# Gated attention outputs turned by VectorE and DMA instead of TensorE, for six of eight heads of the last layer

## Chip, cores and metric

One Trainium2 chip, one of its cores. The metric is the device time of one execution of the whole program in microseconds; lower is better. The median of 3 runs before the change is 2311.38 us (2311.08 to 2311.39).

## What is computed

Two blocks on 256 tokens of 2048 channels. The first is a mixer, a cross attention and a gated feed-forward layer. The second is a convolution layer and then a differential-attention layer, which is the one that matters here:

```python
def _diff_layer(x, k, v, norm_g, w_in, q_norm_g, lam_p, subln_g, w_out, layer_idx):
    ...
    q = _rms_norm(q, q_norm_g) * (DIFF_HEAD_DIM ** -0.5)
    ...
    o = _diff_attention(q, k, v, lam)          # 8 heads, each 2 maps of 128 and 256 values wide
    o = _rms_norm(o, subln_g) * (1.0 - lam_init)
    o = o.reshape(bsz, s, DIFF_V) * jax.nn.silu(z)
    return x + o @ w_out
```

Everything is fp32. The last product, `o @ w_out`, needs the gated output with its 2048 channels along the partitions, while the attention leaves it with the tokens along them, so it has to be turned.

## The kernel before

**Halves and slots.** All large products are walked as one line of 704 "halves" of weights, two blocks of 128 rows by 512 columns each (one product of 32 columns apart). For each half ScalarE rounds the fp32 weights in RAW to fp32r (WHI), VectorE takes the remainder (WLO; GpSimd does so for a part of the convolution layer), and TensorE multiplies: high by high, high by low and low by high, for two halves of the tokens and two blocks, 12 matmuls of 128x512. There are four buffers of WHI and WLO, so ScalarE may round half h+3 when TensorE is through with half h-1 (`ahead`, line 493). SyncE loads the weights, four pieces of two halves ahead.

**Steps behind halves.** Everything else is written out by hand as steps that each engine carries out, in its own program order, behind a given half: `put` for the whole kernel, and for the last layer `diff_put(s, ...)`, which counts slots from the first half of "dq" (line 643 on). Slots 0 to 31 are the query product, 32 to 63 the product for the gate z, and 64 to 71 the first column block of the output product "do". At a slot an engine first prepares weights (rounding or remainder of half s+3) and then does its steps; TensorE multiplies half s and then does its steps. Behind slots 39, 47, 55 and 63 ScalarE also evicts a block of z with Silu into DZ, after its steps.

**Attention.** There are 16 units n (head n//2, token half n%2). The steps of unit n lie at slots from 12+3n on: `ds` the scores on TensorE; one slot later `dexp`, a maximum on VectorE and two exponentials on ScalarE; at +2 `dp`, three VectorE instructions that mix the two maps; at +3 `dt`, TensorE turns the result; +4 `dcopy` on ScalarE; +5 `do`, the product with the values; +6 `dsquare`, the squares on ScalarE and then a scale and a power on GpSimd; +7 `dscale`, VectorE writes the scaled output to XD. Scores read queries and keys from DQT and DKT.

**The turn around the change.** Head h is multiplied by its gate on VectorE (`gated`, slot 43 to 67) and one slot later turned (`oT`, slots 44, 47, 50, 53, 59, 62, 66, 68). `oT` is four 128x128 transposes on TensorE (line 100) into a PSUM bank, two ScalarE instructions that scale and round to Ohi, and two VectorE instructions for the remainder Olo. Ohi shares its place with the keys (DKT) and Olo with the queries (DQT). "do" needs chunks 2p and 2p+1 of Ohi and Olo at its part p, that is at slot 64+p.

**The other way of turning.** For several earlier stages the kernel already turns without TensorE: `swap` (VectorE, line 1528) turns a block of 128x512 in 32x32 squares, two instructions of line 117, into a buffer of 4 KB per partition; `move` (line 665) then lets SyncE and GpSimd issue eight DMAs each, within SBUF, that carry the squares to their places (line 138); `moved_hi` and `moved_lo` read them from there. All swaps stand in the list SWAPS, and one waits until the move of the one before has landed. The last swap before the change is that of the first query block.

Of the kernel before, what the change touches and what calls it, by code (L numbers as in the profile page):

```python
# [164 lines left out]
def flat(ap):  # L165
    return ap.rearrange("p a c -> p (a c)")
# [6 lines left out]
def build_program(nc, I, C, out):  # L173
# [4 lines left out]
    def at(name, kb, shape, dt=F32):  # L178
# [4 lines left out]
    X = at("X", 0, [2, D])  # L183
# [8 lines left out]
    AR = 122  # L192
# [80 lines left out]
             "x3": (at("T3", AR + 64, [1024]), at("B3", AR + 68, [1024])),  # L273
             "x4": (at("T4", AR + 80, [1024]), at("B4", AR + 48, [1024])),
             "x5": (at("T5", AR + 80, [1024]), at("B5", AR + 54, [1024])),
             "ff": (at("TF", AR + 80, [1024]), flat(AC))}
    SWAPS = [("x2", 0), ("x2", 1), ("xk", 0), ("x2", 2), ("xk", 1), ("x2", 3), ("xk", 2), ("xk", 3)]
    SWAPS += [("xq", i) for i in range(3)] + [("x3", i) for i in range(4)] + [("ff", i) for i in range(11)] + [("x4", i) for i in range(4)] + [("x5", i) for i in range(4)]
    SWAPS += [("dk", i) for i in range(4)] + [("dq", 0)]

    X5_HOMES = (SWAP["x5"][1], at("B5b", AR + 58, [1024]))

# [3 lines left out]
    def blocks_home(stage, i):  # L286
        if stage == "xk":
            return flat(XK[:, 4 * i:4 * i + 4, :])
        if stage == "x5":
            return X5_HOMES[i % 2][:, :]  # L290
        return SWAP[stage][1][:, :]

    def landing(stage, i):
# [364 lines left out]
    for h in range(8):  # L658
        s = (44, 47, 50, 53, 59, 62, 66, 68)[h]
        diff_put(s - 1, ("gated", h))  # L660
        diff_put(s, ("oT", h))
    for i in range(1, 4):
        put(("dq", i + 1) if i < 3 else ("dz", 0), 0, ("head", "dq", i))

# [466 lines left out]
    def act_program(engine):  # L1131
# [160 lines left out]
        def step(what, *a):  # L1292
# [118 lines left out]
            elif what == "yT":  # L1411
                e.wait_ge(*full(("down", 6, 3)))
                for q in (4 * k, 4 * k + 2):
                    e.wait_ge(*of("pa", ("yT", q)))
                    e.activation(YT[:, q:q + 2, PAD:PAD + T], kc(pa.ap(("yT", q))[:, :])).then_inc(*done("yT", q))
            elif what == "zT":
                for q in (4 * k, 4 * k + 2):
                    e.wait_ge(*of("pa", ("zT", q)))
                    e.activation(ZT[:, q:q + 2, 0:T], kc(pa.ap(("zT", q))[:, :])).then_inc(*done("zT", q))
            elif what == "tap0":  # L1420
                tap0(k)
            elif what == "copy":
                e.wait_ge(*of("tap", 2 * k + 1, CW - 1))
                e.activation(CV[:, 2 * k:2 * k + 2, :], kc(pb.ap(("taps", k))[:, :])).then_inc(*done("copied", k))
            elif what == "provisional":
                e.wait_ge(*of("pa", ("provisional",)))
                e.activation(MU[:, :], pa.ap(("provisional",))[:, 0:T], scale=1.0 / (4 * P)).then_inc(*done("provisional", 0))
            elif what == "square":
                e.wait_ge(*(of("centred_pool", k) if k < 2 else of("centred", k)))
                if k > 2:  # L1430
                    e.wait_ge(*of("added", k - 2))
                o = SQ[:, 2 * (k % 2):2 * (k % 2) + 2, :] if k else SSQ
                e.activation(o, CV[:, 2 * k:2 * k + 2, :], AF.Square).then_inc(*done("squared", k))
            elif what == "stats":
                dm = cols("dm", 2)
                e.wait_ge(*of("variance", 0))
                e.activation(DIAG[:, 0, :], IDN[:, :], scale=dm[:, 0:1])
                e.activation(DIAG[:, 1, :], IDN[:, :], scale=dm[:, 1:2]).then_inc(*done("diag_mean", 0))
            elif what == "spread_rstd":
                rs = cols("rs", 2)  # L1440
                e.wait_ge(*of("rstd", "y"))
                e.activation(DIAG[:, 2, :], IDN[:, :], scale=rs[:, 0:1])
                e.activation(DIAG[:, 3, :], IDN[:, :], scale=rs[:, 1:2]).then_inc(*done("diag_rstd", 0))
            elif what == "silu_y":
                silu_y(k)
            elif what == "y_hi":
                y_hi(k)
            elif what == "x5T":
                e.wait_ge(*full(("cz", 3)))
                moved_hi("x5", k)  # L1450
            elif what == "x5bT":
                moved_hi("x5b", k)
            elif what == "mask":
                e.wait_ge(*of("d_mrow", 0))
                e.activation(MASK, MROW).then_inc(*done("mask", 0))
            elif what == "dexp":
                nk = P * (k % 2 + 1)
                v, o = pa.ap(("ds", k))[:, 0:2 * nk].rearrange("p (m c) -> p m c", m=2), diff_exps(k)
                mx, sm = cols(("dmax", k % 4), 2), cols(("dsum", k % 4), 2)
                if k > 1:  # L1460
                    e.wait_ge(*of("pa", ("dt", k - 2)))
                e.wait_ge(*of("diff_max", k))
                for mp in range(2):
                    i = e.activation(o[:, mp, 0:nk], v[:, mp, :], AF.Exp, bias=mx[:, mp:mp + 1], accum_out=sm[:, mp:mp + 1])
                i.then_inc(*done("diff_exp", k))
            elif what == "dcopy":
                nk = P * (k % 2 + 1)
                if k > 1:
                    e.wait_ge(*of("pb", ("do", k - 2)))
                e.wait_ge(*of("pa", ("dt", k)))  # L1470
                e.activation(diff_turned(k)[:, 0:nk], pa.ap(("dt", k))[:, 0:nk]).then_inc(*done("diff_T", k))
            elif what == "dsquare":
                h, t = k // 2, k % 2
                e.wait_ge(*of("pb", ("do", k)))
                e.activation(XD[:, t, h * T:(h + 1) * T], pb.ap(("do", k))[:, 0:T], AF.Square,
                             accum_out=cols(("dss", k % 4), 1)[:, 0:1]).then_inc(*done("diff_sq", k))
            elif what == "oT":
                e.wait_ge(*of("sg", 0))
                t_hi("o", 2 * k, pa, "pa", ("o", 2 * k))

        e.wait_ge(*of("half", 0))
        e.activation(cols("begin", 1), HALF[:, 0:1]).then_inc(*done("act_begun", 0))
# [18 lines left out]
    def dve_program(engine):  # L1501
# [26 lines left out]
        def swap(stage, i):  # L1528
            n = SWAPS.index((stage, i))
            if n:  # L1530
                for landed_blocks in landing(*SWAPS[n - 1]):
                    e.wait_ge(*landed_blocks)
            home_free = {("xq", 0): full(("xkv", 7)), ("dk", 0): full(("co", 3)), ("dq", 0): full(("dv", 3)),
                         ("x2", 0): of("mem_sq", 1), ("x3", 0): of("pa", ("att", 3)), ("x5", 0): of("pa", ("zT", 14)), ("ff", 0): of("pa", ("qxT", 14))}
            if i == 0 and (stage, i) in home_free:
                e.wait_ge(*home_free[stage, i])
            made = {"ff": "up", "xk": "xkv", "xq": "xq", "dk": "dk", "dq": "dq"}
            e.wait_ge(*(evicted((made[stage], i)) if stage in made else of("x_add", stage, i, 1)))
            for t in range(2):
                a = {"ff": AC, "xk": NT, "xq": NT, "dk": ND, "dq": ND}[stage][:, t, :] if stage in made else X[:, t, i * 512:(i + 1) * 512]  # L1540
                m = e.turn_blocks(turned_blocks(stage, t), a.rearrange("p (k q c) -> p q k c", k=4, q=4))
            m.then_inc(*done("swapped", stage, i))

# [337 lines left out]
        def step(what, *a):  # L1881
# [163 lines left out]
            elif what == "dexp":  # L2045
                nk = P * (k % 2 + 1)
                e.wait_ge(*of("pa", ("ds", k)))
                e.reduce(cols(("dmax", k % 4), 2), pa.ap(("ds", k))[:, 0:2 * nk].rearrange("p (m c) -> p m c", m=2), AL.max, negate=True) \
                    .then_inc(*done("diff_max", k))
            elif what == "dp":  # L2050
                diff_weights(k)
            elif what == "dscale":
                h, t = k // 2, k % 2
                e.wait_ge(*of("rstd", ("diff", k)))
                e.tensor_scalar(XD[:, t, h * T:(h + 1) * T], pb.ap(("do", k))[:, 0:T], cols(("r", ("diff", k % 4)), 1)[:, 0:1], AL.mult) \
                    .then_inc(*done("diff_o", k))
            elif what == "gated":
                s = slice(k * T, (k + 1) * T)
                e.wait_ge(*of("diff_o", 2 * k + 1))
                e.wait_ge(*evicted(("dz", k // 2)))  # L2060
                e.tensor_tensor(XD[:, 0, s], XD[:, 0, s], DZ[:, 0, s], AL.mult)
                e.tensor_tensor(XD[:, 1, s], XD[:, 1, s], DZ[:, 1, s], AL.mult).then_inc(*done("gated", k))
            elif what == "oT":
                e.wait_ge(*of("sg", 0))
                t_lo("o", 2 * k, pa, ("o", 2 * k))

        begun = 0
        for h, (name, part, last) in enumerate(line):
# [338 lines left out]
```

## Time and profile before

| | us |
|---|---|
| median of 3 runs | 2311.38 |
| lowest, highest | 2311.08, 2311.39 |
| the profiled execution: its time | 2312.47 |
| the profiled execution: its span | 2310.6 |

The profile is of one execution. Its span reaches from the first to the last instruction; the 1.87 us between span and time lie around it. The page lists busy time per engine, the span in 40 slices, the DMA queues, the chain of work that ended last, and groups of instructions. Times in the rows further down are microseconds from the start of the span. In this trace slot 44 ends at about 2155, slot 64 begins at about 2219, and the last matmul ends at about 2307.5.

### The profile page before, as it was taken

How to read it: one execution, taken by the hardware profiler on the slowest of the kernel's cores; microseconds unless marked ns; L12 is line 12 of the kernel's file. 1: busy time of each engine (PE TensorE's matmuls, PEld its weight loads, DVE VectorE, ACT ScalarE, POOL GpSimd, SP SyncE). 2: the span in 40 equal slices, each digit the busy share in tenths (PEclk: the TensorE clock that was granted, in tenths of full speed). 3: DMA queues.
4: the chain of work that ended last, by engine and by line, in shares of the span. 5: the costliest groups of instructions: out<-in, count | busy, mean ns of one | idle time of the engine just before them, and what ended most of it. 6: DMA issues, size and time to landing. Idle time of an engine off the chain costs nothing.

```text
span 2310.6 us, 26507 instructions
## 1 busy us (share of the span) xinstructions
PE 2303.0 (100%) x10418; PEld 1898.8 (82%) x10418; DVE 1422.9 (62%) x1939; ACT 1118.1 (48%) x1452; POOL 494.0 (21%) x567
## 2 busy tenths in 40 slices
PE   9999999999999999999999999999999999999999
PEld 7778888888888888888888888888888888888887
DVE  6687756644556555554455555679994765466564
ACT  6444555544335444443344444544556554444653
POOL 1001011300102100100000101159987322022100
PEclk9999999999999999999999999999999999999999
DMA  9566466765546666565566566655655676554454
GB/s 335 191 195 201 149 225 208 235 222 184 171 147 222 206 228 199 192 227 186 197 201 201 196 219 212 201 197 168 200 182 182 199 241 218 187 187 152 158 172 138
DMA packets 252380, 458.17 MB, mean 198 GB/s; under 512 B 19658, under 2 KB 39813, under 8 KB 251552
## 3 DMA queue, kind: packets, MB, share of 16 engines
q1 hardware_dynamic: 238608, 432.13, 56.2%
q0 software_dynamic: 13648, 24.35, 3.8%
q8 instruction: 82, 1.34, 0.2%
q14 instruction: 42, 0.34, 0.0%
HBM read 431.79 MB, written 2.10 MB: 188 GB/s over the span
## 4 chain that ended last, share of the span: by engine, by line
PE 95%; DVE 2%; ACT 1%; DMA 1%; issue 1%; SPq 0%; POOL 0%; DVEq 0%; ACTq 0%
PE ps L97 94%; PE ps L100 1%; DVE WLO L109 1%; ACT WHI L103 0%; DMA RAW<-in_w_in 0%; SPq L138 0%; DMA B<-T 0%; POOL B L138 0%; DVE MIX L109 0%; DMA B5b<-T 0%; ACT ps L103 0%; DVE T L117 0%; ACT L103 0%; DVE UU L109 0%; DVE HS L109 0%
## 5 line engine op out<-in xcount | busy, mean ns | idle before, releaser
L109 DVE TENSOR_TENSOR WLO<-RAW,WHI 128x1024 fp32r<-128x1024 f32 x701 | 851.5, 1221 | 700.6 <-ACT WHI L103 697.3
L103 ACT ACTIVATE WHI<-RAW 128x1024 fp32r<-128x1024 f32 x793 | 836.2, 1059 | 867.7 <-PE ps L97 861.8
L97 PE MATMUL ps<-WHI,Ahi 128*128 128x512 f32 x1904 | 750.8, 395 | 0.3 <-DVE WLO L109 0.3
L97 PE MATMUL ps<-WHI,Alo 128*128 128x512 f32 x1904 | 741.7, 390 | 0.0
L97 PE MATMUL ps<-WLO,Ahi 128*128 128x512 f32 x1904 | 741.4, 390 | 0.0
L97 PEld LDWEIGHTS ps<-WHI,Ahi 128*128 128x128 f32 x1904 | 358.6, 188 | 76.5 <-issue 2.3
L97 PEld LDWEIGHTS ps<-WLO,Ahi 128*128 128x128 f32 x1904 | 358.7, 188 | 75.4 <-issue 2.3
L97 PEld LDWEIGHTS ps<-WHI,Alo 128*128 128x128 f32 x1904 | 358.5, 188 | 75.0
L109 POOL TENSOR_TENSOR WLO<-RAW,WHI 128x1024 fp32r<-128x1024 f32 x92 | 219.0, 2417 | 53.0 <-ACT WHI L103 52.6
L120 DVE SCALAR_TENSOR_TENSOR ps<-YT,GC,ps 128x256 f32<-128x256 f32 x480 | 188.8, 482 | 8.0 <-ACT ps L103 8.0
L138 POOL DMA_DIRECT2D AC<-TF x88 | 46.4, 535 | 562.0 <-DVE TF L117 559.1
L97 PE MATMUL ps<-WHI,Bhi 128*128 128x512 f32 x384 | 150.3, 391 | 0.0
L97 PE MATMUL ps<-WHI,Blo 128*128 128x512 f32 x384 | 149.4, 389 | 0.0
L97 PE MATMUL ps<-WLO,Bhi 128*128 128x512 f32 x384 | 149.4, 389 | 0.0
L114 POOL TENSOR_SCALAR ST<-ST 128x1 f32<-128x1 f32 (+3 forms) x53 | 21.8, 412 | 549.4 <-DVE ST L123 258.6
L97 PE MATMUL ps<-WHI,Fhi 128*128 128x512 f32 x352 | 136.9, 389 | 0.0
L97 PE MATMUL ps<-WLO,Fhi 128*128 128x512 f32 x352 | 136.9, 389 | 0.0
L97 PE MATMUL ps<-WHI,Flo 128*128 128x512 f32 x352 | 136.9, 389 | 0.0
L138 POOL DMA_DIRECT2D B<-T x112 | 59.4, 538 | 218.5 <-DVE T L117 206.7
L97 PE MATMUL ps<-WHI,Dhi 128*128 128x512 f32 x256 | 102.6, 401 | 0.0
L97 PE MATMUL ps<-WHI,Dlo 128*128 128x512 f32 x256 | 100.1, 391 | 0.0
L97 PE MATMUL ps<-WLO,Dhi 128*128 128x512 f32 x256 | 99.9, 390 | 0.0
(328 smaller groups left out, 2216.3 us busy)
## 6 DMA issues: line engine op xcount, KB each, us to landing
RAW<-in_w_gate_up SPq DMA_DIRECT2D x88, 1024.0 KB, 5.1
RAW<-in_a_w_in SPq DMA_DIRECT2D x48, 1024.0 KB, 5.1
RAW<-in_w_down SPq DMA_DIRECT2D x44, 1024.0 KB, 5.0
RAW<-in_w_in SPq DMA_DIRECT2D x39, 1024.0 KB, 5.2
RAW<-in_w_xkv SPq DMA_DIRECT2D x32, 1024.0 KB, 5.6
RAW<-in_w_kv SPq DMA_DIRECT2D x32, 1024.0 KB, 5.7
RAW<-in_b_w_in SPq DMA_DIRECT2D x32, 1024.0 KB, 5.4
RAW<-in_w_out SPq DMA_DIRECT2D x16, 1024.0 KB, 5.0
```

Source lines behind the costliest of these rows:

```text
L97: return self.e.matmul(o, l, r, start=start, stop=stop, skip_group_check=True)
L100: return self.e.transpose(o, i, ident)
L103: return self.e.activation(o, i, func, scale=scale, **kw)
L109: return self.e.tensor_tensor(o, a, b, op)
L114: return self.e.tensor_scalar(o, a, s1, s2, op0, op1)
L120: return self.e.scalar_tensor_tensor(out=o, in0=a, scalar=s, in1=b, op0=op0, op1=op1)
L138: return self.e.dma_start(o, i)
```

## The change

Heads 0 to 5 are no longer turned on TensorE. At slots 47, 53 and 62 a swap "o" 0, 1 and 2 takes two gated heads (512 columns of XD) each, as soon as the second of them is gated. The squares lie in a buffer TO (where ND was) and are moved to places that queries and keys no longer in use have left: DQT 8 to 11, DKT 8 to 11 and DQT 12 to 15. Two and three slots later `moved_hi` and `moved_lo` read four chunks in two steps. SyncE and GpSimd issue the moves at the slot of the swap, because their programs carry out every "swap" step. Heads 6 and 7 stay on TensorE.

```diff
-             "ff": (at("TF", AR + 80, [1024]), flat(AC))}
+             "ff": (at("TF", AR + 80, [1024]), flat(AC)), "o": (at("TO", AR + 80, [1024]), None)}
...
-    SWAPS += [("dk", i) for i in range(4)] + [("dq", 0)]
+    SWAPS += [("dk", i) for i in range(4)] + [("dq", 0)] + [("o", i) for i in range(3)]
...
+        if stage == "o":
+            return flat((DQT[:, 8:12, :], DKT[:, 8:12, :], DQT[:, 12:16, :])[i])
...
     for h in range(8):
         s = (44, 47, 50, 53, 59, 62, 66, 68)[h]
         diff_put(s - 1, ("gated", h))
-        diff_put(s, ("oT", h))
+        if h >= 6:
+            diff_put(s, ("oT", h))
+        elif h % 2:
+            diff_put(s, ("swap", "o", h // 2))
+            diff_put(s + 2, ("oM", 2 * h - 2))
+            diff_put(s + 3, ("oM", 2 * h))
...
+            elif what == "oM":
+                e.wait_ge(*of("sg", 0))
+                moved_hi("o", k)
...
-                         ("x2", 0): of("mem_sq", 1), ...}
+                         ("x2", 0): of("mem_sq", 1), ...,
+                         ("o", 0): of("pa", ("dqT", 14))}
...
-            e.wait_ge(*(evicted((made[stage], i)) if stage in made else of("x_add", stage, i, 1)))
+            if stage == "o":
+                e.wait_ge(*of("gated", 2 * i + 1))
+                e.wait_ge(*of("pa", ("ds", (11, 11, 15)[i])))
+            else:
+                e.wait_ge(*(evicted((made[stage], i)) if stage in made else of("x_add", stage, i, 1)))
...
-                a = {...}[stage][:, t, :] if stage in made else X[:, t, i * 512:(i + 1) * 512]
+                a = {...}[stage][:, t, :] if stage in made \
+                    else (XD if stage == "o" else X)[:, t, i * 512:(i + 1) * 512]
...
+            elif what == "oM":
+                e.wait_ge(*of("sg", 0))
+                moved_lo("o", k)
```

## Rows read from the trace of the kernel before

**Rows 1.** The page: busy us by engine, and TensorE's granted clock by slice.

```profile
PE 2303.0 (100%) x10418; PEld 1898.8 (82%) x10418; DVE 1422.9 (62%) x1939; ACT 1118.1 (48%) x1452; POOL 494.0 (21%) x567
...
PEclk9999999999999999999999999999999999999999
```

**Rows 2.** Whom TensorE waited for, whole span: us in total, times, longest.

```profile
PE ps L97 <- DVE WLO L109: 1.6, 2, 1.3
PE ps L97 <- issue: 1.1, 1, 1.1
```

**Rows 3.** Chain that ended last, from 1980 us: start, us, what (L100 transposes).

```profile
2155.67 0.44 PE ps L100 x4
...
2233.96 73.51 PE ps L97 x324
```

**Rows 4.** Instructions on XD: TensorE transposes, duration ns min/median/max.

```profile
L100 PE MATMUL ps<-IDN,XD x32: 270/272/275, 2155.5 to 2233.7; 128*128 128x128 f32 x32
```

**Rows 5.** Timeline of DVE, POOL and SP at the last swap: start, us, engine.

```profile
2038.75 1.30 DVE L117 STREAM_TRANSPOSE TDQ<-ND 128x512 f32<-128x512 f32 x2
...
2040.35 4.30 POOL L138 DMA_DIRECT2D BDQ<-TDQ  x8 [3.15 <-DVE TDQ L117]
...
2040.08 5.95 SPq L138 DMA_DIRECT2D BDQ<-TDQ  x8
...
2047.37 1.14 DVE L114 TENSOR_SCALAR DQT<-BDQ,GC 128x256 f32<-128x256 f32 x4 [2.80 <-DMA BDQ<-TDQ]
```

**Rows 6.** Timeline of VectorE, slots 47 to 50.

```profile
2165.86 0.48 DVE L120 SCALAR_TENSOR_TENSOR TMP<-TMP,ST 128x256 f32<-128x256 f32 x1
2167.21 0.88 DVE L120 SCALAR_TENSOR_TENSOR Olo<-ps,ST,Ohi 128x256 fp32r<-128x256 f32 x2 [0.87 <-ACT Ohi L103]
...
2173.72 0.48 DVE L113 TENSOR_SCALAR XD<-ps,ST 128x256 f32<-128x256 f32 x1 [0.44 <-POOL ST L109]
2174.12 0.41 DVE L123 TENSOR_REDUCE ST<-ps 128x2 f32<-128x256 f32 x1
...
2177.50 0.15 DVE L132 RECIPROCAL ST<-ST 128x1 f32<-128x1 f32 x1
```

**Rows 7.** GpSimd: a scale and a power; all powers from 2140 to 2240 (ns min/median/max).

```profile
2158.45 0.93 POOL L114 TENSOR_SCALAR ST<-ST 128x1 f32<-128x1 f32 x1 [5.97 <-ACT XD L103]
2159.47 0.55 POOL L109 TENSOR_TENSOR ST<-ST 128x1 f32<-128x1 f32 x1
...
L109 POOL TENSOR_TENSOR ST<-ST x8: 548/550/1507, 2147.9 to 2220.0; 128x1 f32<-128x1 f32 x8
```

**Rows 8.** Timeline of ScalarE: moved chunks of an earlier stage, then slots 49 to 56.

```profile
1851.12 0.91 ACT L103 ACTIVATE Ahi<-B5b,GC 128x256 fp32r<-128x256 f32 x2 [1.92 <-DMA B5b<-T]
...
2174.57 0.37 ACT L103 ACTIVATE GC<-ps,ST 128x128 f32<-128x128 f32 x1 [0.98 <-DVE ST L123]
...
2175.27 1.05 ACT L103 ACTIVATE WHI<-RAW 128x1024 fp32r<-128x1024 f32 x1
...
2193.58 1.28 ACT L103 ACT_TABLE_LOAD   x1
...
2196.03 2.00 ACT L103 ACTIVATE WHI<-RAW 128x1024 fp32r<-128x1024 f32 x2
```

**Rows 9.** Timeline of TensorE: `dt` of units 12 and 14, `oT` of head 6.

```profile
2179.23 0.28 PE L100 MATMUL ps<-IDN,GC 128*128 128x128 f32 x1
...
2199.30 0.27 PE L100 MATMUL ps<-IDN,GC 128*128 128x128 f32 x1
...
2227.43 0.60 PE L100 MATMUL ps<-IDN,XD 128*128 128x128 f32 x4
```

**Rows 10.** Timeline of VectorE: end of slot 56 (`dp` of unit 14), slots 62 and 65.

```profile
2198.72 0.35 DVE L120 SCALAR_TENSOR_TENSOR GC<-GC,ST 128x128 f32<-128x128 f32 x1
...
2213.78 1.23 DVE L109 TENSOR_TENSOR WLO<-RAW,WHI 128x1024 fp32r<-128x1024 f32 x1 [0.62 <-ACT WHI L103]
...
2225.08 0.75 DVE L109 TENSOR_TENSOR XD<-XD,DZ 128x256 f32<-128x256 f32 x2
```

More of the change, by code:

```diff
@@ L1533, in swap @@
             home_free = {("xq", 0): full(("xkv", 7)), ("dk", 0): full(("co", 3)), ("dq", 0): full(("dv", 3)),
-                         ("x2", 0): of("mem_sq", 1), ("x3", 0): of("pa", ("att", 3)), ("x5", 0): of("pa", ("zT", 14)), ("ff", 0): of("pa", ("qxT", 14))}
+                         ("x2", 0): of("mem_sq", 1), ("x3", 0): of("pa", ("att", 3)), ("x5", 0): of("pa", ("zT", 14)), ("ff", 0): of("pa", ("qxT", 14)),
+                         ("o", 0): of("pa", ("dqT", 14))}
             if i == 0 and (stage, i) in home_free:
@@ L1537, in swap @@
             made = {"ff": "up", "xk": "xkv", "xq": "xq", "dk": "dk", "dq": "dq"}
-            e.wait_ge(*(evicted((made[stage], i)) if stage in made else of("x_add", stage, i, 1)))
+            if stage == "o":
[3 more added lines that the diff above has]
+                e.wait_ge(*(evicted((made[stage], i)) if stage in made else of("x_add", stage, i, 1)))
             for t in range(2):
-                a = {"ff": AC, "xk": NT, "xq": NT, "dk": ND, "dq": ND}[stage][:, t, :] if stage in made else X[:, t, i * 512:(i + 1) * 512]
+                a = {"ff": AC, "xk": NT, "xq": NT, "dk": ND, "dq": ND}[stage][:, t, :] if stage in made \
+                    else (XD if stage == "o" else X)[:, t, i * 512:(i + 1) * 512]
                 m = e.turn_blocks(turned_blocks(stage, t), a.rearrange("p (k q c) -> p q k c", k=4, q=4))
```

## Prediction, made before the changed kernel was run

> **What bounds the kernel.** I read the page first. TensorE is busy over the whole span, VectorE 62%, ScalarE 48%, and the granted clock is full in every slice, its 2.4 GHz level [rows 1]. The list of waits then shows that TensorE hardly waits for anyone: 1.6 us for VectorE and 1.1 us for "issue" in 2310.6 us [rows 2]. So every instruction taken off TensorE comes off the end, and every new wait of TensorE is added to it. The chain of waits gives the price of the transposes in question: the four of a head hold TensorE for 0.44 us between weight matmuls [rows 3]. The timelines around the last existing swap [rows 5] and around slots 47 to 66 [rows 6 to 10] show what the other engines will be asked to do instead, and how early they are today.
>
> **Removed from TensorE.** Six heads at four transposes at 0.11 us: 6 x 0.44 = 2.64 us [rows 3]. The same transposes have a duration of 272 ns each [rows 4], but they overlap one another and the matmuls around them. The chain counts what they delay, and I take it.
>
> The Trainium skill (TensorE: Matmul & The Clock Gate, Part 4: PE-mode transpose) puts a 128x128 transpose at about 275 ns in one kernel, which is the row's duration. By that figure the gain would be 6.6 us instead of 2.64.
>
> **Removed from ScalarE and VectorE, and put back.** Two roundings and two remainders per head stay as they are, only their source moves from PSUM to SBUF: 0.91 us for two roundings of moved chunks [rows 8], 0.88 us for two remainders [rows 6]. New are two VectorE turns per swap, 1.30 us [rows 5], three times. VectorE has the time on average; the question is what stands behind them.
>
> **Added on the queues.** Per swap GpSimd issues eight DMAs, 4.30 us, beginning 0.3 us after the turn; SyncE issues eight too, 5.95 us, and the data is in place 7.3 us after the turn ended (2040.05 to 2047.37) [rows 5]. On SyncE only weight loads are queued behind them, four pieces or eight halves of 12 matmuls ahead, 8 x 12 x 73.51/324 = 21.8 us [rows 3]; 5.95 us of lateness fits into that, so I cost it at nothing. On GpSimd the scale and power of `dsquare` stand behind them. These take 1.57 us with their gap (2158.45 to 2160.02) [rows 7]. So GpSimd delivers at +4.6 +1.6 = 6.2 us after the turn at the earliest, and VectorE's `dscale`, one slot after `dsquare`, waits for it. That `dscale` stands ahead of the maximum of a later unit.
>
> The last existing swap cost TensorE the 1.1 us of "issue" in [rows 2], at the time when VectorE waited for the moved queries of [rows 5], on which the first scores depend. A swap can stall TensorE.
>
> **Swap 0 (slot 47).** TensorE runs 0.44 us earlier here, after one `oT` less, so `dp` of unit 11 ends at 2165.85 (was 2165.86 + 0.45 [rows 6]), and the turn ends at 2167.15 = A. Then: dscale at A+6.2; maximum 0.40 later; exponentials 0.45 after that, A+7.05; they take 0.70 (2174.57 to 2175.27 [rows 8]), A+7.75. Now the new rounding (landed since A+7.3) 0.87, A+8.6. VectorE, in order, holds at the remainder of the moved chunks for it: 0.88, A+9.5. Then `gated` 0.7, the weights' remainder 1.15 [rows 10] (both a little under the row, since the next instruction starts before the end of the last), three instructions of `dp` 0.8 [rows 6, 10]: A+12.1 = 2179.25. TensorE's `dt` of unit 12 was at 2179.23 [rows 9]; three `oT` less it would be there at 2177.9. **Stall 1.3 us.**
>
> **Swap 1 (slot 53).** VectorE now works without a gap from 2179.2: remainder 0.88, two weights' remainders 2.3, dscale 0.4, maximum 0.7; exponentials 0.9, rounding 1.1, remainder 1.15, `dp` of unit 13 0.9, turn 1.3: B = 2188.8. Up to the moved rounding all is as above, B+8.6. But this is slot 55, where ScalarE must still load a table and evict z, together 2.45 (2193.58 to 2196.03), before it rounds the weights, 0.96 [rows 8], and VectorE takes its remainder, 1.15, and `dp` of unit 14, 0.8: B+14.1 = 2202.9. `dt` of unit 14 was at 2199.30 [rows 9], without further stall now 2198.9. **Stall 4.0 us.** Before, this chain ended at 2199.07 [rows 10], 0.2 us before TensorE came to it.
>
> **Swap 2 (slot 62).** All is 3.6 us later, less 0.44 for head 4: remainder at 2213.78 + 3.15 [rows 10] = 2216.9, turn ends at 2219.4, landed at 2226.7. ScalarE rounds the moved chunks to 2227.5, the weights to 2228.5; VectorE then the weights' remainder 2229.6, the second moved one 2230.5, `gated` of head 6 2231.3. TensorE's `oT` of head 6 was at 2227.43 [rows 9], now ready at 2230.1. **Stall 1.2 us.** From there on only full halves follow, with three buffers of lead, and the 324 matmuls of the tail [rows 3] keep their pace.
>
> **Sum.** -2.64 + 1.3 + 4.0 + 1.2 = +3.9 us. For the profiled execution 2312.47 + 3.9 = 2316.4 us; the median of the runs is 1.09 lower than that execution, so 2311.38 + 3.9 = **2315.3 us**. A measurement of this kernel tells 0.2% from nothing, 4.6 us: the bounds are 2306.8 and 2316.0, and the forecast is within them, near the upper.
>
> Two prices are not shown in this place. A burst of eight issues on GpSimd while VectorE works: between the 4.30 us of GpSimd and the 5.95 us of SyncE [rows 5]; I take GpSimd's own. GpSimd's scale and power right behind a burst: between 1.57 and 0.93 + 0.09 + 1.51 = 2.5 us [rows 7]; I take the first, as the median power took 0.55 us.
>
> **Rivals.**
> *The stalls are covered* (chance 0.20). If VectorE's lead absorbs the waits, as around the 39 earlier swaps, where TensorE's waits are 2.7 us in all [rows 2], only the gain remains, with at most half the stalls: 2308.7 to 2311.9 us. For it speaks that every step has a slot of slack by design; against it, that `dt` of unit 14 has next to none and that GpSimd was idle beside the earlier swaps [rows 5], with no `dscale` behind them.
> *GpSimd behind its DMAs is slow* (chance 0.22, slower). If the power takes 1.51 instead of 0.55 us [rows 7] after a burst of issues, swaps 0 and 1 both pay 0.9 us more: 2315.3 + 1.8 = 2317.1 us. It decides from 0.7 us of extra stall in the sum on. Against it: of the eight powers of these slots the median took 0.55 [rows 7].
> *The clock falls* (chance 0.03, slower). TensorE would idle 4.0 us in one go, three times more than anywhere before. If it goes on at 1.2 GHz for one half, whose 12 matmuls take 12 x 73.51/324 = 2.7 us [rows 3] at full clock, that adds 2.7 us: 2318.0. No stretch of this trace shows the lower level, so only a stall as long as that can tell.
> The Trainium skill (TensorE: Matmul & The Clock Gate, Why this matters for your kernels) asks to keep gaps between bursts of matmuls short, or the clock goes back to half; the trace before has no gap that would test it.
> *A transpose costs its full duration* (chance 0.03, faster). 24 x 0.272 = 6.5 us [rows 4] with the stalls covered gives 2304.9 us. Against it: the chain's 0.44 for four [rows 3].
> *The change does nothing* (0.02): if heads were still turned on TensorE, 2311.4. The diff leaves no room for it.
>
> **How the numbers follow.** The forecast case holds 0.50: +1.8 to +5.5 us, 2313.2 to 2316.9, of which a tenth of all chance lies above 2316.0. Slower: 0.22 + 0.03 + 0.10 = 0.35. Faster by over 0.2%: 0.03. Within: 0.62. The range runs from 2309.5, into the covered case, to 2318.2, past the slow GpSimd.
>
> **What would show it.** In the profile after: TensorE's transposes on XD fall from 32 to 8. TensorE waits for VectorE's TMP/GC (the mixed maps) at slots 51 and 57 with gaps of about 1.3 and 4 us, and for XD before head 6 with about 1.2. GpSimd has three bursts of eight DMAs of 4.3 us each in front of a late scale and power; VectorE's XD from `dscale` waits for GpSimd some 2 to 4 us. The step is wrong if GpSimd's burst ends well before `dscale` is due, if the moved chunks land much later than 7.3 us (then the landing, not GpSimd, sets it), or if the gaps sum to less than 2.6 us, which makes the kernel faster. If TensorE waits for WLO instead, the lead of three halves was used up, and the sum is wrong upwards.

## The result, and the profile after

The changed kernel takes 2316.15 us (median of 13 runs, 2313.84 to 2317.92) against 2311.39 us (13 runs, 2310.72 to 2312.92): +4.76 us, a ratio of 1.0021 with a 95% interval of 1.0014 to 1.0028. The forecast was 2315.3 us, in a range of 2309.5 to 2318.2. The measured median lies 0.15 us above 2316.0, the upper bound of what the prediction counted as no change; it had given 0.35 to the side above it. The runs of the changed kernel lie over 4.1 us, those before over 2.2 us; a part of that spread has a cause of its own, below.

The page after, busy us by engine, beside [rows 1]:

```profile
PE 2301.9 (100%) x10394; PEld 1895.7 (82%) x10394; DVE 1425.8 (62%) x1945; ACT 1117.9 (48%) x1452; POOL 504.3 (22%) x591
```

TensorE has 24 instructions less, VectorE 6 more, GpSimd 24 more, its half of the moves. Busy time barely moves. The instructions on XD after, beside [rows 4]:

```profile
L100 PE MATMUL ps<-IDN,XD x8: 270/273/328, 2230.1 to 2236.4; 128*128 128x128 f32 x8
```

Of 32 transposes 8 are left, so the change does what it says. Whom TensorE waits for from 2140 us on, after (us in total, times, longest); before there was the last of the three lines alone:

```profile
PE ps L100 <- DVE GC L120: 3.7, 2, 3.1
PE ps L100 <- DVE XD L109: 1.2, 1, 1.2
PE ps L100 <- DVE TMP L120: 0.2, 1, 0.2
```

Three new waits (two of the first line, one of the second), at the three places of the forecast. The profiled execution of this kernel took 2315.23 us with a span of 2313.3. Its start is not comparable to the microsecond: at unit 9, ahead of all changed slots, it is already 1.64 us ahead of the one before (2146.70 against 2148.34 us), which is chance of a single execution: the one profiled before lies 1.09 us above the median of its kernel, this one 0.92 below. So I count from that transpose to the final addition (chain of waits, after, then the same before):

```profile
2146.70 0.44 PE ps L100 x2
...
2310.20 0.69 DVE X L109
```

```profile
2148.34 0.44 PE ps L100 x2
...
2307.49 0.69 DVE X L109
```

That is 2310.20 - 2146.70 = 163.50 us. Before it was 2307.49 - 2148.34 = 159.15 us: +4.35 us within the changed stretch.

TensorE's timeline after, the units 12 and 14 and head 6, beside [rows 9]:

```profile
2177.07 0.33 PE L100 MATMUL ps<-IDN,GC 128*128 128x128 f32 x1 [0.60 <-DVE GC L120]
2177.23 1.03 PE L97 MATMUL ps<-DKT,DQT 128*128 128x256 f32 x4
...
2199.97 0.47 PE L100 MATMUL ps<-IDN,GC 128*128 128x128 f32 x1 [3.05 <-DVE GC L120]
2200.24 1.91 PE L97 MATMUL ps<-DKT,DQT 128*128 128x256 f32 x4
2201.59 0.78 PE L97 MATMUL ps<-MASK 128*128 128x256 f32 x1
2202.17 0.63 PE L97 MATMUL ps<-WHI,Dhi 128*128 128x512 f32 x1
2202.59 0.53 PE L97 MATMUL ps<-WLO,Dhi 128*128 128x512 f32 x1
2202.96 0.40 PE L97 MATMUL ps<-WHI,Dlo 128*128 128x512 f32 x1
...
2230.09 0.66 PE L100 MATMUL ps<-IDN,XD 128*128 128x128 f32 x4 [1.23 <-DVE XD L109]
```

Taken against the places of [rows 9], 1.64 us earlier and 0.44 us less per head removed, and with what came before taken off, the three stalls are 0.8, 3.3 and 1.4 us. That is some 0.2 us more than the idle times of 0.60, 3.05 and 1.23: matmuls that otherwise start 0.23 us apart and take 0.39 do not overlap across a wait.

Behind the long one there is something more. The four score matmuls after unit 14 take 1.91 us where they took 1.03 us elsewhere (at 2177.23 us, behind unit 12). Windows of five microseconds, after (columns: busy us and count of PE, PEld, DVE, ACT, POOL, then granted clock, DMA share, GB/s):

```profile
2195.00:2200.00 5.00, 1.95 (x10) 1.26 (x9) 2.29 (x6) 4.99 (x10) 0.00 (x0) 0.95 0.25 96
2200.00:2205.00 5.00, 5.00 (x17) 4.16 (x18) 4.64 (x8) 3.43 (x8) 2.03 (x2) 0.71 0.77 230
2205.00:2210.00 5.00, 5.00 (x23) 4.12 (x23) 2.72 (x5) 2.51 (x5) 0.55 (x2) 1.00 0.50 193
```

The granted clock is 0.71 between 2200 and 2205 us: a part of it at 1.2 GHz, after 3 us in which TensorE did nothing, and back at 2.4 GHz by 2205. From unit 14 to the third weight matmul behind it pass 2202.96 - 2199.97 = 2.99 us. Before, it was 2200.86 - 2199.30 = 1.56:

```profile
2199.30 0.27 PE L100 MATMUL ps<-IDN,GC 128*128 128x128 f32 x1
...
2200.86 0.40 PE L97 MATMUL ps<-WHI,Dlo 128*128 128x512 f32 x1
```

**The fall of the clock costs 1.4 us.** The idling before it does not make the difference: in the profiled execution of experiment 5, below, TensorE idles 2.54 us in this place, the clock is 1.00 in the windows around it, and the same stretch takes 2200.20 - 2198.58 = 1.62 us. The page's line by slices shows nothing of it, as a slice is 58 us long. By the Trainium skill (TensorE: Matmul & The Clock Gate, Why this matters for your kernels) long gaps between bursts of matmuls put the clock back to half; this trace agrees, with 0.71 behind a gap of 3.05 us.

The sum within the trace: 24 transposes -2.6 (measured below), stalls +5.5, clock +1.4, together +4.3, against +4.35. The stalls are themselves differences of places, so up to head 6 the sum closes by its making. What the trace shows beside it is that the idle times fit the stalls, and that nothing is added behind head 6.

Now the chain behind the 3.3 us, on three engines (timelines after, slots 53 to 56):

```profile
2185.10 1.30 DVE L117 STREAM_TRANSPOSE TO<-XD 128x512 f32<-128x512 f32 x2
...
2191.97 0.48 DVE L113 TENSOR_SCALAR XD<-ps,ST 128x256 f32<-128x256 f32 x1 [2.52 <-POOL ST L109]
2192.37 0.41 DVE L123 TENSOR_REDUCE ST<-ps 128x2 f32<-128x256 f32 x1
2194.46 0.88 DVE L120 SCALAR_TENSOR_TENSOR Olo<-DKT,ST,Ohi 128x256 fp32r<-128x256 f32 x2 [1.67 <-ACT Ohi L103]
2197.98 1.22 DVE L109 TENSOR_TENSOR WLO<-RAW,WHI 128x1024 fp32r<-128x1024 f32 x1 [2.64 <-ACT WHI L103]
```

```profile
2186.69 4.30 POOL L138 DMA_DIRECT2D DKT<-TO  x8 [4.21 <-DVE TO L117]
2191.03 0.27 POOL L114 TENSOR_SCALAR ST<-ST 128x1 f32<-128x1 f32 x1
2191.38 0.56 POOL L109 TENSOR_TENSOR ST<-ST 128x1 f32<-128x1 f32 x1
```

```profile
2193.52 0.90 ACT L103 ACTIVATE Ohi<-DKT,ST 128x256 fp32r<-128x256 f32 x2
2194.44 1.28 ACT L103 ACT_TABLE_LOAD   x1
2195.74 1.27 ACT L103 ACTIVATE DZ<-ps,ST 128x512 f32<-128x512 f32 x2
2196.89 1.05 ACT L103 ACTIVATE WHI<-RAW 128x1024 fp32r<-128x1024 f32 x1
```

It reads from top to bottom. The turn ends at 2186.40. GpSimd issues eight DMAs and only then does its scale and power, so VectorE's scaled output waits 2.52 us for it and the maximum of unit 14 comes at 2192.37, 6.0 us after the turn. ScalarE's exponentials (2192.82 to 2193.52) are followed by the moved rounding, then the table and the eviction of z, then the weights of the next half; VectorE waits for each of the two and mixes unit 14 at last, 13.5 us after the turn. The landing is not what ends last here: the moved rounding starts at 2193.52, at once behind the exponentials.

### The profile page after: what moved, and what is told of

Read it like the earlier page. It is cut to its first block, busy times and chain, and to the rows that moved or that the text cites. A ratio compares the mean times of both kernels' runs of the same rounds, so it can differ in the third digit from the quotient of the medians.

```text
span 2313.3 us, 26521 instructions
## 1 busy us (share of the span) xinstructions
PE 2301.9 (100%) x10394; PEld 1895.7 (82%) x10394; DVE 1425.8 (62%) x1945; ACT 1117.9 (48%) x1452; POOL 504.3 (22%) x591
## 4 chain that ended last, share of the span: by engine, by line
PE 93%; DVE 3%; ACT 2%; DMA 1%; issue 1%; POOL 1%; SPq 0%; DVEq 0%; ACTq 0%
PE ps L97 92%; DVE WLO L109 1%; PE ps L100 1%; ACT WHI L103 1%; SPq L138 0%; DMA RAW<-in_w_in 0%; DMA B<-T 0%; ACT L103 0%; POOL DKT L138 0%; POOL DQT L138 0%; DVE TO L117 0%; POOL B L138 0%; DVE MIX L109 0%; DMA DQT<-TO 0%; ACT ps L103 0%
```

## The experiments

All times are medians of 11 runs, beside 21 or 33 runs of the kernel before on the same chip (2311.40, 2311.36 and 2311.21 us in the three groups). Where a kernel leaves work out, as in experiments 2 to 4, its output is not the right one; such kernels serve for the time alone.

**1. The work on the transposes alone.** Kernel before, with this in TensorE's step:

```diff
             elif what == "oT":
                 e.wait_ge(*of("gated", k))
+                if k < 6:
+                    bank, free = pa.banks[len(pa.held) % 2], pa.held[len(pa.held) - 2]
+                    e.wait_ge(*of(*free))
+                    for j in range(2):
+                        for t in range(2):
+                            c = 2 * k + j
+                            e.transpose(bank[:, j * T + t * P:j * T + (t + 1) * P], XD[:, t, c * P:(c + 1) * P], IDN[:, :])
                 turn_nat("o", 2 * k, XD)
```

> The kernel before the change, with the 24 transposes of heads 0 to 5 done twice (the first time into the same bank, overwritten by the second). It measures the price of the removed work by itself. By the chain of waits a head costs 0.44 us (0.42 in the traces of the first experiments): +2.5 to +2.6 us, 2313.9 to 2314.0 us. Rival, that a transpose costs its duration of 272 ns: +6.5 us, 2317.9 us.

Measured 2313.99 us (2313.48 to 2315.54), ratio 1.0012 (1.0003 to 1.002): +2.63 us for 24 transposes, 0.44 us per head. TensorE's timeline shows eight where there were four in 0.60 us:

```profile
2154.12 1.04 PE L100 MATMUL ps<-IDN,XD 128*128 128x128 f32 x8
```

The price is the chain's: four more transposes add 1.04 - 0.60 = 0.44 us. The 272 ns of [rows 4] is the duration of one, of which the next covers more than half. By the Trainium skill's 275 ns (TensorE: Matmul & The Clock Gate, Part 4: PE-mode transpose) it would have been 6.6 us; the number agrees with the row and not with the cost in this place.

**2. The change without its swaps.**

```diff
-            diff_put(s, ("swap", "o", h // 2))
...
-    SWAPS += [("dk", i) for i in range(4)] + [("dq", 0)] + [("o", i) for i in range(3)]
+    SWAPS += [("dk", i) for i in range(4)] + [("dq", 0)]
...
+            if stage == "o":
+                e.wait_ge(*of("gated", k // 4 * 2 + 1))
+                e.wait_ge(*of("pa", ("ds", (11, 11, 15)[k // 4])))
```

> The changed kernel without the three swaps: no VectorE turns, no DMAs; the rounding and remainder of heads 0 to 5 stand in their new slots and read what lies in the places of old keys and queries (so the gated outputs of six heads do not reach the output product). My theory: the gain of the removed transposes is real and shows in full once the waits behind the swaps are gone, 2311.4 - 2.6 = 2308.8 us, no TensorE stall over 0.5 us in slots 44 to 68, and no fall of the granted clock. Rival, that the new places of the roundings alone upset VectorE's order: the stalls of 0.8 and 3.3 us at units 12 and 14 stay in part, 2310 us or more.

Measured 2309.36 us (2308.82 to 2311.01), ratio 0.9991 (0.9982 to 1.0): -2.04 us, 0.6 less than the gain that I expected. TensorE's waits from 2140 us on are the 0.2 us at unit 9 and one new:

```profile
PE ps L100 <- DVE GC L120: 0.4, 1, 0.4
```

So the gain is there, less 0.6 us. The one new wait, 0.44 us of idling and 0.2 around it, accounts for that; as I read it, it is the price of the new place of the roundings at unit 14, in front of the eviction of z. The rest of the loss comes with the swaps.

**3. The turns without the DMAs.**

```diff
     def move(e, stage, i, blocks):
+        if stage == "o":
+            return
...
-            for landed_blocks in landing(home, k // 4):
+            for landed_blocks in (landing(home, k // 4) if stage != "o" else [of("swapped", "o", k // 4)]):
...
-                for landed_blocks in landing(*SWAPS[n - 1]):
+                for landed_blocks in (landing(*SWAPS[n - 1]) if stage != "o" or i == 0 else ()):
```

> The changed kernel with VectorE's turns but without any of the 48 DMAs; the moved roundings wait for the turn alone (six heads' outputs do not reach the product). Theory: the stalls come from GpSimd's burst and the landing, not from VectorE's 1.3 us per swap, so the time is that of the kernel without swaps (2309.4 us) or up to 0.5 us more: 2309.4 to 2309.9 us, clock 1.00. Rival, VectorE as the bound: 2311 us or more, TensorE waiting for VectorE at units 12 and 14 by over 1 us.

Measured 2309.32 us (2308.7 to 2309.93), ratio 0.9991 (0.9982 to 1.0), with the same single wait of 0.4 us. Against experiment 2 VectorE's six turns cost nothing that shows. The whole difference to the changed kernel, 2316.15 - 2309.32 = 6.8 us, is the 48 DMAs: their issue, their landing and what the stall does to the clock.

**4. Without GpSimd's half of the moves.**

```diff
-        return [of(f"d_move{b}", stage, i, 3) for b in range(4)]
+        return [of(f"d_move{b}", stage, i, 3) for b in range(2 if stage == "o" else 4)]
...
-            elif what == "swap":
+            elif what == "swap" and k != "o":
                 move(e, *a, blocks=(2, 3))
```

> The changed kernel without GpSimd's half of the moves: SyncE issues its eight DMAs per swap as before, GpSimd none, and nobody waits for the missing half (half of the squares of six heads are missing). Rival, that GpSimd's scale and power behind its DMAs set the stall: the stalls at units 12 and 14 shrink by about 2 us each and the kernel falls to 2311 to 2312 us. My reading of the trace after: dscale becomes early, but the landing of SyncE's half, 7.3 us after the turn, holds the moved rounding at the same moment as before, so the two waits hide each other and the time stays at 2315 to 2316.5 us with the same stalls of about 0.8, 3.3 and 1.4 us.

Measured 2313.96 us (2312.63 to 2314.46), ratio 1.001 (1.0002 to 1.0019): 2.2 us less than the changed kernel, so the time I named is missed by 1 us, and the rival's by 2. The timeline of VectorE and that of ScalarE in slots 55 and 56 show why it is between them (the turn ends at 2186.70 here):

```profile
2190.07 0.41 DVE L123 TENSOR_REDUCE ST<-ps 128x2 f32<-128x256 f32 x1
2194.09 0.88 DVE L120 SCALAR_TENSOR_TENSOR Olo<-DKT,ST,Ohi 128x256 fp32r<-128x256 f32 x2 [3.61 <-ACT Ohi L103]
```

```profile
2193.15 0.91 ACT L103 ACTIVATE Ohi<-DKT,ST 128x256 fp32r<-128x256 f32 x2 [1.83 <-DMA DKT<-TO]
```

As I read it, the maximum comes 2.6 us earlier after the turn (3.4 instead of 6.0 us) and it hardly helps, because the rounding now waits for the landing. But SyncE's half alone lands 6.45 us after the turn, not 7.3, and the idle times shrink to 0.35 and 2.4 us with none at head 6. In the change the exponentials end 7.1 us after the turn (2193.52), here the landing comes at 6.45. Two waits end within a microsecond of each other; taking one away yields only the difference, and the mix of unit 14 comes 12.9 instead of 13.5 us after the turn.

**5. The roundings one slot later.**

```diff
-            diff_put(s + 2, ("oM", 2 * h - 2))
-            diff_put(s + 3, ("oM", 2 * h))
+            if h < 5:
+                diff_put(s + 3, ("oM", 2 * h - 2))
+                diff_put(s + 4, ("oM", 2 * h))
...
+        if h == 6:
+            diff_put(65, ("oM", 8))
+            diff_put(66, ("oM", 10))
...
+                e.wait_ge(*of("T_lo", "o", 2 * k - 2))
```

> The changed kernel with its swaps where they are, but the moved roundings and remainders one slot later, behind the mixes of units 12 and 14 (slots 50 and 51, 56 and 57) and behind the gating of head 6 (65 and 66). It takes the landing out of the way and leaves GpSimd's burst in front of the scale. By the trace after: the maximum 6.0 us after the turn, exponentials to 7.1, table and eviction 2.45, rounding and remainder of weights 2.1, mix 0.8: unit 14 at 12.5 instead of 13.6 us after the turn, and unit 12 not late at all. Stall 1.9 us at unit 14, none at unit 12, at most 0.3 at head 6: 2311.4 - 2.5 + 1.9 = 2310.8 us (2310.2 to 2311.6). Rival, that the place of the roundings alone made the stalls: 2309.2 us. Rival, that GpSimd's burst alone made them: 2314 us or more.

Measured 2313.3 us (2311.03 to 2314.57), ratio 1.0007 (0.9999 to 1.0016): 2.5 us more than I expected, and outside the range. The waits from 2140 us on are where I said, with the one at unit 12 and the one at head 6 gone and this one left:

```profile
PE ps L100 <- DVE GC L120: 2.5, 1, 2.5
```

It is 2.5 us where I had 1.9, and I had left out the clock: in eight of the 11 runs the mean granted clock is 0.999. Those eight lie at 2312.83 to 2314.57, the other three at 2311.03 (the profiled one), 2311.65 and 2311.70, near the forecast. VectorE's timeline shows the part that is GpSimd's alone, in slot 55:

```profile
2191.37 0.48 DVE L113 TENSOR_SCALAR XD<-ps,ST 128x256 f32<-128x256 f32 x1 [2.81 <-POOL ST L109]
```

So at unit 14 TensorE idles 3.05 us in the change, 2.4 without GpSimd's burst (experiment 4), 2.5 with the roundings behind the mix (here), and 0.4 without any DMA (experiment 3). Neither cause alone accounts for the stall; each hides most of the other.

**6. Without swap 1, and with swap 1 alone.** The first leaves heads 2 and 3 on TensorE, the second all the others (the list SWAPS is shortened to match):

```diff
-        if h >= 6:
+        if h >= 6 or h in (2, 3):
             diff_put(s, ("oT", h))
```

```diff
-        if h >= 6:
+        if h not in (2, 3):
             diff_put(s, ("oT", h))
```

> Heads 2 and 3 are turned on TensorE again as before the change; swaps 0 and 2 stay. Theory: swap 1 carries the long stall (3.3 us) and, behind it, the fall of the clock (1.4 us in the profiled run). Without it -16 transposes 1.76, +0.8 (unit 12) +1.4 (head 6): 2311.8 us (2311 to 2312.5), granted clock 1.00 from slot 44 to the end, and the spread over the runs as small as before the change (2 us or less). Rival, that each swap costs about a third: 2314.5 us.

> Only heads 2 and 3 by swap (slot 53), the other six heads on TensorE. Theory: -0.84 for eight transposes, a stall of about 2.8 us at unit 14 and, in most runs, the fall of the clock behind it, 1.4 us: 2314.7 us (2313.5 to 2315.5), in two levels 1.4 us apart according to the mean granted clock of the run. Rival, each swap costs a third of the loss: 2313 us, and the clock stays.

Without swap 1: 2313.72 us (2313.06 to 2314.81), ratio 1.0011 (1.0002 to 1.002), 1.9 us more than expected and outside the range; the rival's 2314.5 is nearer. TensorE's waits from 2150 us on:

```profile
PE ps L100 <- DVE XD L109: 2.9, 2, 1.5
```

One of the two is the known one at head 6. The other, 1.51 us, is new and stands at slot 50: with head 2 back on TensorE, its transposes wait for its gating, which VectorE does behind the remainder of swap 0. I had carried over only the stall at unit 12; the same lateness meets whatever stands next. It costs 1.7 us in place of the 0.8 at unit 12, which is 0.9 of the 1.9 us; the stall at head 6 is 0.4 longer than I had it. The clock is 1.00 in all 11 runs, and the spread is 1.75 us, as expected.

Swap 1 alone: 2314.45 us (2313.28 to 2315.15), ratio 1.0013 (1.0004 to 1.0022), as expected and 1.5 us above the rival, so swap 1 carries more than a third. It waits 2.6 us at unit 14, and the window behind it shows the clock:

```profile
2200.00:2205.00 5.00, 4.77 (x16) 3.93 (x17) 4.90 (x9) 3.43 (x8) 2.03 (x2) 0.67 0.66 220
```

The four runs with a mean clock of 1.000 lie at 2313.28 to 2314.64 (median 2313.5), the seven with 0.999 at 2314.14 to 2315.15 (median 2314.7): 1.2 us apart. The two levels overlap, since runs of one level differ by as much. Above the transposes that are saved, swap 1 alone costs 3.24 + 0.88 = 4.1 us, swaps 0 and 2 cost 2.32 + 1.76 = 4.1, and all three together 4.76 + 2.64 = 7.4: the costs of the swaps are not independent of each other.

**7. Other slots for the same work.**

```diff
-        s = (44, 47, 50, 53, 59, 62, 66, 68)[h]
+        s = (44, 47, 50, 53, 59, 60, 66, 68)[h]
...
-            diff_put(s, ("swap", "o", h // 2))
-            diff_put(s + 2, ("oM", 2 * h - 2))
-            diff_put(s + 3, ("oM", 2 * h))
+            w, m0, m1 = {1: (48, 51, 53), 3: (54, 57, 59), 5: (60, 63, 64)}[h]
+            diff_put(w, ("swap", "o", h // 2))
+            diff_put(m0, ("oM", 2 * h - 2))
+            diff_put(m1, ("oM", 2 * h))
```

> The same work as in the change at other slots: each swap one slot later, right behind GpSimd's scale and power (48, 54, and 60 with head 5 gated at 59), the moved roundings where VectorE has neither a maximum nor a mix ahead of TensorE (51, 53; 57, 59; 63, 64). Theory: all three stalls go, the gain of 2.6 us is left: 2308.8 us (2308 to 2310), clock 1.00. Rival, that the transfers themselves or VectorE's six extra turns cost time wherever they stand: 2311 us or more.

Measured 2309.99 us (2309.52 to 2310.44), ratio 0.9994 (0.9985 to 1.0003). The same transposes, turns and 48 DMAs, and 6.2 us less than the change. Nothing is left but one wait of 0.6 us at head 6, where I had expected none. This is also what speaks against the transfers or the turns as such: they are all still there. The next kernel has (43, 46, 49, 52, 57, 57, 64, 67) as slots of `gated`, swap 2 at 58, its roundings at 61 and 62, and a wait for the remainder of the chunks before, since the places overlap in time:

> The slots of e4_shifted, and the third pair earlier: heads 4 and 5 gated at slot 57, swap 2 at 58, its roundings at 61 and 62, head 6 gated at 64, so that neither the landing nor the eviction of z behind slot 63 stands in front of head 6. Theory: the last 0.6 us stall goes too, 2310.0 - 0.8 = 2309.2 us or a little less (2308.8 to 2309.4), no stall over 0.3 us in slots 44 to 68 besides the 0.2 us at unit 9. Rival, that the landing at slot 61 or swap 2's burst in front of the scale of unit 14 makes a new wait: 2310 us or more.

Measured 2309.22 us (2308.5 to 2311.61), ratio 0.9991 (0.9982 to 1.0): TensorE waits for no one behind unit 9, and -2.14 us of the possible 2.5 to 2.6 are there. Then the last two heads, gated together at slot 64 and moved to the place of the used values:

```diff
+    DVH = at("DVH", AR + 48, [4, T])
...
+            w, m0, m1 = {1: (48, 51, 53), 3: (54, 57, 59), 5: (58, 61, 62), 7: (64, 67, 68)}[h]
...
+                e.wait_ge(*(of("pa", ("ds", (11, 11, 15)[i])) if i < 3 else of("pb", ("do", 15))))
```

> As e7_all_waits_gone, and heads 6 and 7 too by VectorE and DMA: both gated at slot 64, swap 3 there, moved to the place of the used values, rounded at slots 67 and 68. The output product needs chunks 12 at slot 70, 14 at 71. Theory: another 2 x 0.42 us less, 2308.3 us (2308 to 2308.8). Rival, that the landing, 7.4 us or 2.7 halves after the turn, comes too late for the rounding and remainder before slot 70: 2309.5 us or more, with TensorE waiting for Olo or for the weights' remainder.

Measured 2308.2 us (2307.52 to 2309.03), ratio 0.9986 (0.9977 to 0.9994): **3.2 us faster than the kernel before and 8 us faster than the change.** All its 11 runs lie below the lowest of the 33 beside them (2310.60). For the two kernels before it the intervals reach 1.0 or past it, so their gains rest on the traces as much as on the times. TensorE's waits over the whole span hold nothing behind unit 9, whose 0.2 us were there before:

```profile
PE ps L97 <- DVE WLO L109: 1.7, 2, 1.5
PE ps L97 <- POOL ONE L135: 1.0, 1, 1.0
PE ps L97 <- DVE KN L106: 0.3, 1, 0.3
PE ps L97 <- issue: 0.3, 1, 0.3
PE ps L100 <- DVE TMP L120: 0.2, 1, 0.2
```

ScalarE does wait there for the last landing, 4.42 us, with nothing of TensorE's behind it but halves whose weights are ready:

```profile
2229.78 0.91 ACT L103 ACTIVATE Ohi<-DVH,ST 128x256 fp32r<-128x256 f32 x2 [4.42 <-DMA DVH<-TO]
```

## Why the prediction was right, and where its sizes were off

The sign, the places and, roughly, the size hold. Point by point:

- **The removed work**, 2.64 us: 2.63 by doubling it (experiment 1), and 2.57 within the same stretch of the trace of the second kernel of experiment 7, which has no new wait (2303.20 - 2146.62 = 156.58 against 159.15 us). Right.
- **The turns on VectorE at nothing**: right, experiment 3.
- **SyncE's eight DMAs at nothing**: after the change TensorE waits for no WLO and ScalarE for no RAW in slots 44 to 71. Right.
- **Swap 0**: 1.3 us forecast, 0.8 in the trace. The term at fault is GpSimd's scale and power behind its burst, for which I took 1.57 us; from their start to VectorE's scaled output it is 0.94 (2191.03 to 2191.97 at swap 1, 2170.12 to 2171.06 at swap 0). The rival that made them slow was the wrong way round.
- **Swap 1**: 4.0 forecast, 3.3 in the trace. The mix was put at 14.1 us after the turn and came at 13.5, 0.6 us of it by the same term. Experiment 4 shows that the two waits I had put side by side, GpSimd at 6.2 (in the trace 5.6) and the landing at 7.3 us, do hide each other.
- **Swap 2**: 1.2 forecast, 1.4 in the trace. The landing was at 7.5 us after the turn instead of 7.3.
- **The clock** was a rival with a chance of 0.03 and came with the forecast case: ten of the 13 runs of the changed kernel have a mean clock of 0.999. I had reserved it for a stall of 4 us, and priced it at 2.7 us where it costs 1.4. This is the one event of the result that the forecast case did not contain. By the mean clock of the runs it falls in 33 of the 46 runs of the four kernels with a stall of 2.4 to 3.1 us of idle time (the change, experiments 4, 5 and swap 1 alone), and in one of the 77 runs of the seven kernels whose waits in this stretch are 1.5 us or less. The waits are those of the one profiled execution of each kernel, and a mean of 0.999 shows only a loss of more than a microsecond or so of full clock (0.0005 of 2313 us), so a shorter fall would not be counted.

- **The covered case** was weighed with TensorE's waits as "2.7 us in all". [rows 2] holds the two largest lines only; the whole list before adds up to 4.2 us, of which 1.0 is at the very start. It changes no term of the sum.

So two errors of opposite sign, stalls too long by 1 us and a clock held steady at a price of 1.4, bring 3.9 us to the 4.3 of the trace; that they nearly cancel is luck. The 0.4 us from there to the 4.76 of the medians is not explained. The three runs at clock 1.000 have a median of 2314.93 us, 3.5 us above the kernel before.

Not settled: experiment 6 without swap 1 is 0.5 us above what its trace adds up to (+1.8 us within the stretch, +2.3 in the medians), and its cause stays open.

## What to carry to other kernels

Where TensorE is busy all the time, a step taken off it gains its place in the chain, not its duration, and that gain survives only if what replaces it is behind nothing that TensorE needs next. Moving work is then a question of slots: here the same instructions cost 4.8 us or gained 2.1 us. In the one case the burst of DMA issues stands in front of a one-column operation on the same queue and the roundings in front of a mix that TensorE needs, in the other they stand behind them. Where two waits end together, as the burst and the landing do here, look at both before one is removed.

## What was not expected of the hardware

After a stall of TensorE of some 2.5 us the granted clock is at 1.2 GHz when it resumes, in most executions and not in all. The traces of the change (3.05 us of idling) and of swap 1 alone (2.6) show it, those of experiments 4 and 5 (2.4 and 2.5) show 1.00 around it, though eight of the 11 runs of each have a mean of 0.999. The fall costs 1.2 to 1.9 us by the levels of the runs (1.7 in the changed kernel, 1.5 in experiment 4, 1.9 in experiment 5, 1.2 with swap 1 alone) and 1.4 us in the trace of the change. Two levels within one kernel widen its spread: 4.1 us for the change and 3.5 for experiment 5. But the spread alone is no sign of it: experiment 4 and swap 1 alone have 1.8 and 1.9 us, the kernels without a long stall 0.9 to 3.1. GpSimd's scale and power of one column took 0.9 us right behind a burst of DMA issues (three times in the change, as 2191.03 to 2191.94), where most of those after a wait in the trace before took 1.6 to 2.5. That is no rule: after a wait of 3.3 us they took 0.9 as well (experiment 3, 2184.37 to 2185.27).
